# Two RMS norms of a one-core decoder layer: last output tiles and first products by halves of the tokens

## The chip, the cores and the metric

The kernel runs on one core of a Trainium2 chip. The metric is the device time of one execution in microseconds (us), from the first to the last instruction with what lies around them. Before the change the median of three runs is 1109.05 us (1107.43 to 1109.75).

## What is computed

The input x has 512 tokens of 1024 channels. Every product is in float32 accuracy.

```python
h = modulate(rms_norm(x, norm_ffn1), shift0, scale0)
x = x + 0.5 * gate0 * swiglu(h, w_ffn1_in, w_ffn1_out)      # D_FF = 2816
h = modulate(rms_norm(x, norm_mix), shift1, scale1)         # "norm 1" below
u_pool, q_lat, kv_lat, k_rope, g_pool, g_mla = split(h @ w_in)
...                                                         # pooling branch, latent attention, gates
x = x + gate1 * (merged @ w_out)
h = modulate(rms_norm(x, norm_ffn2), shift2, scale2)        # "norm 2" below
x = x + 0.5 * gate2 * swiglu(h, w_ffn2_in, w_ffn2_out)
```

`rms_norm` divides each token by the root of the mean of its squares over all 1024 channels. So a token can be normalised only when all its channels are complete.

## The kernel before

**Layout.** Activations lie with channels on the 128 partitions and tokens along the free axis: x, h_hi and h_lo are 8 tiles (index m or k) of 128 channels x 512 tokens. Each float32 value is split into a high and a low part, and every product is three TensorE matmuls (L433 to L435): high x high, high x low, low x high. Weights stream from HBM in chunks through two slots, w_raw, w_hi, w_lo [0] and [1]. ScalarE makes w_hi (L762, `split`), VectorE w_lo (L1098). A chunk can be split only when TensorE has finished with the chunk before it in the same slot.

**Order.** Each engine runs its own list of instructions, written out by hand, strictly in order. Semaphores link the lists: `wait_ge(sem, n)` stops an engine until another has counted that far, and everything behind it on that engine stops too. `lo_done` counts split chunks, `pe_used` chunks that TensorE has finished, `out_evac` tiles of x that are updated, `lat_ready` finished groups of latent products.

**The stretch around norm 1.** FFN 1 ends with the down projection. It makes the 8 tiles of x one after another (`down`). Tile m takes two chunks of 11 weight tiles (half 0 in slot 0, half 1 in slot 1): 2 x 11 x 3 = 66 matmuls of 512 columns. VectorE adds the result to x (L1592), ScalarE squares it (L771), GpSimd adds the squares up in ssq; VectorE adds the last square (L1116). Then TensorE sums over the partitions (L445: four matmuls of one column, one for each 128 tokens; float32, shown as two each), VectorE forms the variance (L1120), ScalarE the root (L775), VectorE the inverse root with one Newton step (L1125 to L1130) and a diagonal matrix (diag, L1137). TensorE spreads it over all partitions (L451, float32, 512 columns). For each m VectorE scales x (L1153), ScalarE adds the shift to give h_hi (L783), VectorE gives h_lo (L1161). `scaled` has two buffers. The first products behind it are the latents: three column groups cg (256, 256 and 160 columns) times four blocks of 128 tokens, here with h as the loaded operand and the weights as the moving one. Group 0 takes the k tiles as they come; groups 0 and 1 together are 192 matmuls of 256 columns. Chunk 0 of the mixer is split during the last down tile, chunk 1 (`mix_split(1)`) after the norm.

**The stretch around norm 2.** The output projection of the mixer makes the tiles of x with 24 matmuls each, two tiles to a chunk (`for c in range(4)`, evacuation L1517). The same chain follows, and then the up projection of FFN 2: chunk j gives one gate and one up tile, 2 x 8 x 3 = 48 matmuls of 512 columns. Its chunk 0 is split before norm 2, chunk 1 after it. After each chunk ScalarE takes silu (L980), VectorE multiplies (L1529), ScalarE and VectorE split the result (L982, L1531), and ScalarE and VectorE split the next chunk into the free slot.

**SP's queue** loads weights as slots come free; behind `stat_ready` of norm 1 it loads the mixer's constants.

## Time and profile before

| | |
|---|---|
| median of three runs | 1109.05 us (1107.43 to 1109.75) |
| the profiled execution | 1108.44 us |
| its span | 1106.3 us, 12576 instructions |
| TensorE matmul (PE) | 1061.5 us busy, 96% |
| VectorE (DVE) | 523.7 us, 47% |
| ScalarE (ACT) | 368.3 us, 33% |
| GpSimd (POOL) | 71.6 us, 6% |

The profile is of one execution. All its times count from the start of the span. PE's busy time counts overlapping matmuls once. "Idle before" is how long the engine stood before an instruction, and the name behind the arrow is what released it. In the view by stretch a row gives the stretch (us from the span's start), its length, then busy us and count for PE, PEld (weight load), DVE, ACT and POOL, then the granted TensorE clock (1.00 is 2.4 GHz, 0.50 is 1.2 GHz), the DMA share and GB/s. In the view in order of time a row gives start, duration, engine, line and operation.

### The profile page before, as it was taken

To read this page: it belongs to the slowest core of one execution; us is meant where nothing else is said; L and a number is where in the kernel's file an instruction comes from. 1 tells how busy PE (TensorE), PEld (TensorE's weight loads), DVE (VectorE), ACT (ScalarE), POOL (GpSimd) and SP (SyncE) were. 2 spreads that over 40 slices of the span, in tenths; PEclk is the share of its full clock that TensorE was granted. 3 is DMA by queue.
4 is the path that set the end of the run, shared out by engine and by line. 5 is a ranking of instruction groups with operands and counts; after the bars stand their busy time and mean duration, and the time that the engine had idled before them with its cause. 6 is when DMAs were issued, how large, how long until landed. Compare 5 with 4: busy or idle time off the path is not lost.

```text
span 1106.3 us, 12576 instructions
## 1 busy us (share of the span) xinstructions
PE 1061.5 (96%) x4860; PEld 874.5 (79%) x4860; DVE 523.7 (47%) x669; ACT 368.3 (33%) x498; POOL 71.6 (6%) x58
## 2 busy tenths in 40 slices
PE   3999999999999979979999999979999999999998
PEld 2888888888888869768788887858888888888886
DVE  5765564655553262758565455363323333322221
ACT  6532223232121232564444443232322323221110
POOL 0000000000000000850100004200000000000000
PEclk9999999999999989999999999989999999999999
DMA  9764545454763212222121222313232222222222
GB/s 353 293 249 157 224 164 217 176 192 157 245 238 104 102 51 97 91 73 79 39 76 38 76 75 78 114 38 114 76 114 81 109 91 98 90 79 87 95 86 94
DMA packets 28874, 138.56 MB, mean 125 GB/s; under 512 B 3248, under 2 KB 3504, under 8 KB 20912
## 3 DMA queue, kind: packets, MB, share of 16 engines
q1 hardware_dynamic: 28848, 138.23, 34.9%
q8 instruction: 15, 0.25, 0.1%
q14 instruction: 11, 0.09, 0.0%
HBM read 136.12 MB, written 2.10 MB: 125 GB/s over the span
## 4 chain that ended last, share of the span: by engine, by line
PE 90%; POOL 3%; DVE 3%; ACT 2%; DMA 1%; issue 1%; SPq 1%; ACTq 0%; DVEq 0%; POOLq 0%
PE bank L433 29%; PE bank L434 28%; PE bank L435 28%; PE bank L676 2%; POOL window L1674 1%; DMA ada_first<-w_ada 1%; PE bank L691 1%; ACT w_hi L762 1%; POOL window L1679 1%; PE bank L664 1%; POOL u_pad L1680 1%; DVE w_lo L1098 1%; POOL h L1703 0%; PE bank L451 0%; DVE mvar L1306 0%
## 5 line engine op out<-in xcount | busy, mean ns | idle before, releaser
L433 PE MATMUL bank<-h_hi,w_hi 128*128 128x512 f32 x928 | 365.8, 394 | 6.4 <-DVE h_lo L1205 2.8
L435 PE MATMUL bank<-h_lo,w_hi 128*128 128x512 f32 x928 | 363.0, 391 | 0.0
L434 PE MATMUL bank<-h_hi,w_lo 128*128 128x512 f32 x928 | 363.0, 391 | 0.0
L1098 DVE TENSOR_TENSOR w_lo<-w_raw,w_hi 128x2048 fp32r<-128x2048 f32 (+3 forms) x96 | 198.6, 2068 | 172.7 <-ACT w_hi L762 172.5
L433 PEld LDWEIGHTS bank<-h_hi,w_hi 128*128 128x128 f32 x928 | 175.3, 189 | 47.2 <-issue 6.1
L762 ACT ACTIVATE w_hi<-w_raw 128x2048 fp32r<-128x2048 f32 (+3 forms) x96 | 164.6, 1715 | 124.4 <-PE bank L435 72.2
L435 PEld LDWEIGHTS bank<-h_lo,w_hi 128*128 128x128 f32 x928 | 175.3, 189 | 37.3
L434 PEld LDWEIGHTS bank<-h_hi,w_lo 128*128 128x128 f32 x928 | 175.4, 189 | 35.8
L433 PE MATMUL bank<-act_hi,w_hi 128*128 128x512 f32 x352 | 139.2, 396 | 0.0
L434 PE MATMUL bank<-act_hi,w_lo 128*128 128x512 f32 x352 | 139.2, 396 | 0.0
L435 PE MATMUL bank<-act_lo,w_hi 128*128 128x512 f32 x352 | 139.2, 396 | 0.0
L980 ACT ACTIVATE scaled<-bank 128x512 f32<-128x512 f32 x44 | 26.3, 597 | 279.7 <-PE bank L435 279.7
L1529 DVE TENSOR_TENSOR scaled<-scaled,bank 128x512 f32<-128x512 f32 x44 | 30.3, 688 | 167.5 <-ACT scaled L980 167.5
L435 PEld LDWEIGHTS bank<-act_lo,w_hi 128*128 128x128 f32 x352 | 66.1, 188 | 16.0
L434 PEld LDWEIGHTS bank<-act_hi,w_lo 128*128 128x128 f32 x352 | 66.1, 188 | 16.0
L433 PEld LDWEIGHTS bank<-act_hi,w_hi 128*128 128x128 f32 x352 | 66.1, 188 | 16.0
L1103 DVE CUSTOM_DVE_ANT_0 ada_raw<-ada_raw,c_wide,const_sb 128x1024 f32<-128x1024 f32 x56 | 69.7, 1280 | 2.9 <-DMA ada_raw<-w_ada 2.9
L1531 DVE TENSOR_TENSOR act_lo<-scaled,act_hi 128x512 fp32r<-128x512 f32 (+1 forms) x44 | 30.5, 693 | 36.3 <-ACT act_hi L982 36.3
L1592 DVE SCALAR_TENSOR_TENSOR x<-bank,out_gate,x 128x512 f32<-128x512 f32 (+1 forms) x16 | 12.0, 751 | 68.4 <-PE bank L435 68.4
L982 ACT ACTIVATE act_hi<-scaled 128x512 f32 (+1 forms) x44 | 27.8, 632 | 39.6 <-DVE scaled L1529 39.6
L771 ACT ACTIVATE scaled<-x 128x512 f32<-128x512 f32 (+1 forms) x16 | 10.1, 632 | 84.7 <-DVE x L1592 57.2
L433 PE MATMUL bank<-w_hi,h_hi 128*128 128x256 f32 (+1 forms) x96 | 28.1, 293 | 2.6 <-DVE h_lo L1161 2.6
(182 smaller groups left out, 891.5 us busy)
## 6 DMA issues: line engine op xcount, KB each, us to landing
w_raw<-w_ffn_in SPq DMA_DIRECT2D x41, 1024.0 KB, 4.8
ada_raw<-w_ada SPq DMA_DIRECT2D x56, 512.0 KB, 5.4
w_raw<-w_ffn_out SPq DMA_DIRECT2D x32, 704.0 KB, 4.0
w_raw<-w_mix SPq DMA_DIRECT2D x21, 1024.0 KB, 4.8
ada_first<-w_ada SPq DMA_DIRECT2D x16, 512.0 KB, 12.7
w_raw<-w_ffn_in SPq DMA_DIRECT2D x6, 512.0 KB, 12.8
x_tok<-x_rows SPq DMA_DIRECT2D x4, 512.0 KB, 6.8
x<-x_t SPq DMA_DIRECT2D x4, 512.0 KB, 5.6
```

What stands on the lines that cost most here:

```text
L433: nc.tensor.matmul(dst, a_hi, b_hi, start=start, stop=False)
L434: nc.tensor.matmul(dst, a_lo, b_hi, start=False, stop=False)
L435: return nc.tensor.matmul(dst, a_hi, b_lo, start=False, stop=stop)
L676: nc.tensor.matmul(bank[qt][:, 0:(qt + 1) * P], q_now[0:HEAD, toks(qt)], k_t[0:HEAD, bass.ds(h, 1), 0:(qt + 1) * P], start=True, stop=False)
L762: nc.scalar.activation(w_hi[slot][:, 0:size], w_raw[slot][:, 0:size], ACT.Copy).then_inc(hi_done, 1)
L980: nc.scalar.activation(silu_g, bank[banks[0]][:, :], ACT.Silu).then_inc(silu_done, 1)
L982: nc.scalar.activation(act_hi[f][:, bass.ds(j, 1), :], prod, ACT.Copy).then_inc(act_hi_done, 1)
L1098: nc.vector.tensor_tensor(w_lo[slot][:, 0:size], w_raw[slot][:, 0:size], w_hi[slot][:, 0:size].bitcast(F32), ALU.subtract).then_inc(lo_don ...
L1103: nc.vector.tensor_tensor_reduce(out=raw, in0=raw, in1=c_wide[:, :], scale=1.0, scalar=bias_ada[:, col:col + 1], op0=ALU.mult, op1=ALU.add ...
L1529: nc.vector.tensor_tensor(prod, silu_g, bank[banks[1]][:, :], ALU.mult).then_inc(gu_evac, 1)
L1531: nc.vector.tensor_tensor(act_lo[f][:, bass.ds(j, 1), :], prod.unsqueeze(1), act_hi[f][:, bass.ds(j, 1), :].bitcast(F32), ALU.subtract)\
L1592: nc.vector.scalar_tensor_tensor(out=xm, in0=bank[4 + s // 2][:, :].unsqueeze(1), scalar=out_gate[:, bass.ds(m, 1)], in1=xm, op0=ALU.mult, ...
```

## The change

The tokens are cut into two halves of 256 (hf 0 and 1).

- The last down tile of FFN 1 (m = 7) and the last two tiles of the output projection (m = 6, 7) are made for half 0 first, then for half 1, each in a bank of its own.
- GpSimd adds up only the squares of the tiles before them. The squares of the halved tiles go to `sq_last`, and TensorE adds them in the sum over the partitions (`norm_sum`), which is made for each half. `norm_wide` spreads each half. Sum and spread of half 0 stand between products of half 1's tiles; those of half 1 between the first products that follow the norm.
- The first two latent groups, and the first two up chunks of FFN 2, take half 0 first and then half 1.
- ScalarE and VectorE work on 128 x 256. Their lists around the norms are written out anew (`norm_mix`, `norm_ffn2`), with the splits of mixer chunks 0 (as two parts, `mix_first`) and 1, and of up chunk 1, between the steps.
- Slots count as free at other points: mixer chunk 0 after 6 groups of latent products. SP loads the mixer's constants after the second sum.

In the diff below the first lists are TensorE's, `high`, `last_square`, `norm_std` are ScalarE's, and the last lists VectorE's; `half_out(m, hf, ...)` is the update of half a tile of x, `norm_var` the variance, `norm_diag` the root's inverse and diag.

```diff
+HALF = S // 2
+LAT_ORDER = [(0, 0), (0, 1), (1, 0), (1, 1), (0, 2), (0, 3), (1, 2), (1, 3), (2, 0), (2, 1), (2, 2), (2, 3)]
+SQUARES_BY_POOL = [0, 7, 13]
+RSTD_BANK = [None, (4, 7), (6, 7)]
...
+        scaled_half = [scaled[:, i // 2, HALF * (i % 2):HALF * (i % 2) + HALF] for i in range(4)]
+        sq_last = place("sq_last", [P, 2, 2, HALF], at=phase_at)
+        diag = place("diag", [P, 2, HALF], at=phase_at + 4096)
...
-            sp.wait_ge(stat_ready, 1)
+            sp.wait_ge(stat_ready, 2)
...
+            def norm_sum(l, hf):
+
+                pe.wait_ge(sq_added, SQUARES_BY_POOL[l])
+                pe.wait_ge(sq_last_done, hf + 1 if l == 1 else 2 + 2 * hf + 2)
+                for t in (2 * hf, 2 * hf + 1):
+                    col = STAT_BANK[:, t:t + 1]
+                    nc.tensor.matmul(col, ssq[:, t * P:(t + 1) * P], ones[:, 0:1], start=True, stop=False)
+                    for mm in range(l):
+                        last = nc.tensor.matmul(col, sq_last[:, hf, mm, t % 2 * P:(t % 2 + 1) * P], ones[:, 0:1],
+                                                start=False, stop=mm == l - 1)
                 last.then_inc(stat_ready, 1)

-            def norm_wide(l):
-                pe.wait_ge(diag_ready, l)
-                nc.tensor.matmul(bank[4][:, :], ones, diag, start=True, stop=True).then_inc(rstd_wide, 1)
+            def norm_wide(l, hf):
+                pe.wait_ge(diag_ready, 2 * (l - 1) + hf + 1)
+                nc.tensor.matmul(bank[RSTD_BANK[l][hf]][:, half_cols(hf)], ones, diag[:, hf, :], start=True, stop=True)\
+                    .then_inc(rstd_wide, 1)
...
+                def up_by_halves():
+
+                    for s in range(2):
+                        pe.wait_ge(lo_done, n0 + s + 1)
+                        pe.wait_ge(gu_evac, NF + s + 1)
+                        for k in range(KD):
+                            if s == 0:
+                                pe.wait_ge(half_ready[0], KD + k + 1)
+                            up_half(s, 0, k)
+                            if s == 0 and k == 2:
+                                norm_sum(2, 1)
+                            if s == 0 and k == 4:
+                                norm_wide(2, 1)
+                    for s in range(2):
+                        for k in range(KD):
+                            if s == 0:
+                                pe.wait_ge(half_ready[1], KD + k + 1)
+                            last = up_half(s, 1, k)
+                        last.then_inc(pe_used, 1)
...
+                def down_last():
+
+                    for half in range(2):
+                        pe.wait_ge(lo_done, n0 + NF + 14 + half + 1)
+                    pe.wait_ge(out_evac, KD + 1 - 1)
+                    for hf in range(2):
+                        for half in range(2):
+                            for k in range(NFH):
+                                cols = half_cols(hf)
+                                last = product(bank[5 + hf][:, cols], w_tile(half, k),
+                                               (act_hi[0][:, half * NFH + k, cols], act_lo[0][:, half * NFH + k, cols]),
+                                               half + k == 0, half * k == NFH - 1)
+                                if hf == 1 and half == 0 and k == 5:
+                                    norm_sum(1, 0)
+                            if hf:
+                                last.then_inc(pe_used, 1)
+                                if half == 0:
+                                    norm_wide(1, 0)
+                            elif half:
+                                last.then_inc(tail_done, 1)
...
+                if f == 0:
+                    with pe.Fori(0, 3) as i:
+                        down(i)
+                    down(3, 1)
+                    down_last()
...
+                for k in range(KD):
+                    if k < 4:
+                        pe.wait_ge(half_lo_done, 2)
+                    else:
+                        chunk(LAT_AT)
+                    pe.wait_ge(half_ready[0], k + 1)
+                    for t in range(2):
+                        lat_part(t, k, 0, t)
+                    if k == 2:
+                        norm_sum(1, 1)
+                    if k == 4:
+                        norm_wide(1, 1)
+                chunk(LAT_AT + 1)
+                for t in range(2):
+                    for k in range(KD):
+                        lat_part(2 + t, k, 1, t)
+                for k in range(KD):
+                    pe.wait_ge(half_ready[1], k + 1)
+                    for t in range(2):
+                        lat_part(4 + t, k, 0, 2 + t)
+                for t in range(2):
+                    for k in range(KD):
+                        lat_part(6 + t, k, 1, 2 + t)
+                chunk(LAT_AT + 2)
+                for t in range(TOK):
+                    pe.wait_ge(lat_evac, t + 1)
+                    for k in range(KD):
+                        lat_part(8 + t, k, 2, t)
...
+                slot = chunk(WOUT_AT + 3)
+                for hf in range(2):
+                    for g in range(2):
+                        pe.wait_ge(out_evac, KD + 6 + 2 * hf + g - 1)
+                        at = (6, 7, 4, 5)[2 * hf + g]
+                        for k in range(KD):
+                            last = product(bank[at][:, half_cols(hf)], w_tile(slot, g * KD + k), h_pair(k, half_cols(hf)),
+                                           k == 0, k == KD - 1)
+                            if (hf, g, k) == (1, 0, 5):
+                                norm_sum(2, 0)
+                            if (hf, g, k) == (1, 1, 2):
+                                norm_wide(2, 0)
+                        if hf and g:
+                            last.then_inc(pe_used, 1)
+                        else:
+                            last.then_inc(tail_done, 1)
...
+            def norm_mix():
+
+                last_square(1, 0, 7, 1)
+                norm_std(1, 0)
+                mix_first(0)
+                high(1, 0, 0)
+                high(1, 0, 1)
+                mix_first(1)
+                high(1, 0, 2)
+                last_square(1, 1, 7, KD + 2)
+                high(1, 0, 3)
+                norm_std(1, 1)
+                high(1, 0, 4)
+                high(1, 0, 5)
+                high(1, 0, 6)
+                mix_split(1)
+                high(1, 0, 7)
...
-                                         bias=mod[:, shift + m:shift + m + 1]).then_inc(h_hi_ready, 1)
+                    high(1, 1, m)
...
+            def scale_in(l, hf, m):
+
+                if m >= 2:
+
+                    dve.wait_ge(half_ready[hf], KD * (l - 1) + m - 1)
+                nc.vector.scalar_tensor_tensor(out=scaled_half[2 * hf + m % 2], in0=x[:, m, half_cols(hf)],
+                                               scalar=gain_mod[:, m:m + 1], in1=bank[RSTD_BANK[l][hf]][:, half_cols(hf)],
+                                               op0=ALU.mult, op1=ALU.mult).then_inc(half_scaled[hf], 1)
+
+            def low(l, hf, m):
+
+                dve.wait_ge(half_scaled[hf], KD * (l - 1) + m + 1)
+                dve.wait_ge(half_high[hf], KD * (l - 1) + m + 1)
+                nc.vector.scalar_tensor_tensor(out=h_lo[:, m, half_cols(hf)], in0=scaled_half[2 * hf + m % 2],
+                                               scalar=mod[:, 3 * KD * l + m:3 * KD * l + m + 1],
+                                               in1=h_hi[:, m, half_cols(hf)].bitcast(F32), op0=ALU.add, op1=ALU.subtract)\
+                    .then_inc(half_ready[hf], 1)
...
+            def norm_mix():
+
+                dve.wait_ge(ada_step, ADA_TILES - ADA_START)
+                gain_cols(1)
+                dve.wait_ge(tail_done, 1)
+                half_out(7, 0, 5, tail_evac)
+                norm_var(1, 0)
+                norm_diag(1, 0)
+                dve.wait_ge(rstd_wide, 1)
+                scale_in(1, 0, 0)
+                scale_in(1, 0, 1)
+                mix_first(0)
+                low(1, 0, 0)
+                scale_in(1, 0, 2)
+                low(1, 0, 1)
+                mix_first(1)
+                dve.wait_ge(pe_used, FFN_CHUNKS)
+                half_out(7, 1, 6, out_evac)
+                scale_in(1, 0, 3)
+                low(1, 0, 2)
+                norm_var(1, 1)
+                scale_in(1, 0, 4)
+                low(1, 0, 3)
+                norm_diag(1, 1)
+                scale_in(1, 0, 5)
+                low(1, 0, 4)
+                scale_in(1, 0, 6)
+                low(1, 0, 5)
+                scale_in(1, 0, 7)
+                low(1, 0, 6)
+                mix_split(1)
+                low(1, 0, 7)
+                dve.wait_ge(rstd_wide, 2)
+                scale_in(1, 1, 0)
...
+                        scale_in(1, 1, m + 1)
+                    low(1, 1, m)
...
+            def norm_ffn2():
+
+                gain_cols(2)
+                for g in range(2):
+                    dve.wait_ge(tail_done, 2 + g)
+                    half_out(6 + g, 0, 6 + g, tail_evac)
+                norm_var(2, 0)
+                norm_diag(2, 0)
+                dve.wait_ge(tail_done, 4)
+                half_out(6, 1, 4, out_evac)
+                dve.wait_ge(rstd_wide, 3)
+                scale_in(2, 0, 0)
+                scale_in(2, 0, 1)
+                low(2, 0, 0)
+                scale_in(2, 0, 2)
+                low(2, 0, 1)
+                dve.wait_ge(pe_used, FFN_CHUNKS + 4)
+                half_out(7, 1, 5, out_evac)
+                scale_in(2, 0, 3)
+                low(2, 0, 2)
+                norm_var(2, 1)
+                scale_in(2, 0, 4)
+                low(2, 0, 3)
+                norm_diag(2, 1)
+                scale_in(2, 0, 5)
+                low(2, 0, 4)
+                scale_in(2, 0, 6)
+                low(2, 0, 5)
+                split(FIRST_CHUNK[1] + 1, 1, IN_ELEMS)
+                scale_in(2, 0, 7)
+                low(2, 0, 6)
+                low(2, 0, 7)
+                dve.wait_ge(rstd_wide, 4)
+                scale_in(2, 1, 0)
```

## Rows read from the trace of the kernel before

**Rows 1.** page: busy us, share of the span, instructions of each engine.

```profile
PE 1061.5 (96%) x4860; PEld 874.5 (79%) x4860; DVE 523.7 (47%) x669; ACT 368.3 (33%) x498; POOL 71.6 (6%) x58
```

**Rows 2.** busy time by stretch, around norm 1 and around norm 2.

```profile
373.63:389.03 15.40, 15.40 (x67) 12.21 (x65) 4.67 (x3) 3.82 (x3) 1.30 (x1) 1.00 0.19 68
389.03:399.26 10.23, 3.27 (x11) 1.50 (x11) 5.31 (x13) 2.31 (x5) 0.47 (x4) 0.76 0.28 85
399.26:424.74 25.48, 25.48 (x193) 25.48 (x194) 15.95 (x31) 9.94 (x15) 0.00 (x0) 0.89 0.24 84
...
716.72:727.61 10.89, 10.89 (x49) 8.82 (x47) 3.71 (x3) 3.07 (x3) 2.60 (x2) 1.00 0.27 96
727.61:737.77 10.16, 3.29 (x12) 1.50 (x11) 5.31 (x13) 3.70 (x6) 0.00 (x0) 0.73 0.00 0
737.77:761.88 24.11, 24.11 (x96) 19.73 (x97) 15.07 (x17) 9.20 (x10) 0.00 (x0) 0.90 0.25 88
```

**Rows 3.** TensorE in order of time in norm 1 (start, us, operation).

```profile
391.52 1.02 PE L445 MATMUL bank<-ones_r,ssq 128*128 128x1 f32 x8 [2.32 <-DVE ssq L1116]
394.56 2.07 PE L451 MATMUL bank<-scaled,ones_r 128*128 128x512 f32 x2 [2.02 <-DVE scaled L1137]
```

**Rows 4.** VectorE and ScalarE in order of time in norm 1.

```profile
389.24 0.75 DVE L1592 SCALAR_TENSOR_TENSOR x<-bank,out_gate,x 128x512 f32<-128x512 f32 x1 [3.40 <-PE bank L435]
...
390.02 0.63 ACT L771 ACTIVATE scaled<-x 128x512 f32<-128x512 f32 x1 [6.51 <-DVE x L1592]
...
393.82 0.69 DVE L1137 TENSOR_TENSOR scaled<-const_sb,rstd 128x512 f32<-128x512 f32 x1
...
396.76 1.41 DVE L1153 SCALAR_TENSOR_TENSOR scaled<-x,gain_mod,bank 128x512 f32<-128x512 f32 x2 [2.17 <-PE bank L451]
...
397.54 1.38 ACT L783 ACTIVATE h_hi<-scaled,mod 128x512 fp32r<-128x512 f32 x2 [4.46 <-DVE scaled L1153]
...
398.37 0.75 DVE L1161 SCALAR_TENSOR_TENSOR h_lo<-scaled,mod,h_hi 128x512 fp32r<-128x512 f32 x1 [0.20 <-ACT h_hi L783]
```

**Rows 5.** the latent products of 256 columns at full clock, by stretch.

```profile
405.00:424.68 19.68, 19.68 (x166) 19.68 (x166) 10.35 (x23) 7.04 (x11) 0.00 (x0) 1.00 0.31 107
```

**Rows 6.** groups by line and form: busy us, mean ns, idle before.

```profile
L1098 DVE TENSOR_TENSOR w_lo<-w_raw,w_hi 128x2048 fp32r<-128x2048 f32 x61 | 141.2, 2315 | 82.3 <-ACT w_hi L762 82.2
L762 ACT ACTIVATE w_hi<-w_raw 128x2048 fp32r<-128x2048 f32 x61 | 116.5, 1910 | 5.2 <-PE bank L435 5.1
...
L783 ACT ACTIVATE h_hi<-scaled,mod 128x512 fp32r<-128x512 f32 x16 | 11.5, 725 | 16.7 <-DVE scaled L1153 16.7
...
L1466 DVE TENSOR_TENSOR p_lo<-bank,p_hi 128x512 fp32r<-128x512 f32 x16 | 10.3, 687 | 26.7 <-ACT p_hi L792 26.7
L792 ACT ACTIVATE p_hi<-bank 128x512 fp32r<-128x512 f32 x16 | 8.7, 599 | 0.0
...
L1466 DVE TENSOR_TENSOR p_lo<-bank,p_hi 128x256 fp32r<-128x256 f32 x8 | 3.3, 415 | 0.0
...
L792 ACT ACTIVATE p_hi<-bank 128x256 fp32r<-128x256 f32 x8 | 3.2, 402 | 0.0
```

**Rows 7.** VectorE and ScalarE in order of time behind down tile 6.

```profile
373.84 0.75 DVE L1592 SCALAR_TENSOR_TENSOR x<-bank,out_gate,x 128x512 f32<-128x512 f32 x1 [4.60 <-PE bank L435]
376.56 1.63 DVE L1098 TENSOR_TENSOR w_lo<-w_raw,w_hi 128x1408 fp32r<-128x1408 f32 x1 [1.97 <-ACT w_hi L762]
...
375.16 1.36 ACT L762 ACTIVATE w_hi<-w_raw 128x1408 fp32r<-128x1408 f32 x1
```

**Rows 8.** ScalarE's silu of up chunk 0, FFN 2, and VectorE's next split.

```profile
751.20 0.60 ACT L980 ACTIVATE scaled<-bank 128x512 f32<-128x512 f32 x1 [3.00 <-PE bank L435]
...
755.10 2.29 DVE L1098 TENSOR_TENSOR w_lo<-w_raw,w_hi 128x2048 fp32r<-128x2048 f32 x1 [1.12 <-ACT w_hi L762]
```

**Rows 9.** TensorE's stop before 494.57, and the stretch 493 to 494.

```profile
494.57 0.77 PE L433 MATMUL bank<-group_hi,w_hi 128*128 128x512 f32 x1 [4.29 <-DVE group_lo L1389]
...
493.00:494.00 1.00, 0.00 (x0) 0.00 (x0) 1.00 (x2) 1.00 (x3) 1.00 (x1) 0.70 0.00 0
```

More of the change, by code:

```diff
@@ L460, in up_part, with up @@
                     return last
-                def up(i, first):
+                def up(i):
                     for s in range(2):
@@ L538, in first_up, with up_half @@
                     last.then_inc(pe_used, 1)
+                def up_half(s, hf, k):
+                    for gu in range(2):
+                        last = product(bank[2 * s + gu][:, half_cols(hf)], w_tile(s, gu * KD + k),
+                                       (h_hi[:, k, half_cols(hf)], h_lo[:, k, half_cols(hf)]), k == 0, k == KD - 1)
+                    return last
+                def up_by_halves():
[16 more added lines that the diff above has]
+                        last.then_inc(pe_used, 1)
                 if f == 0:
@@ L577, in mixer, with lat_part @@
             def mixer():
[L580 to L592 removed]
+                def lat_part(r, k, cg, t):
+                    n = LAT_COLS[cg][1]
+                    last = product(bank[r % 8][:, 0:n], h_pair(k, toks(t)), w_cols((MIX_CHUNK + cg) % 2, k * n, n),
+                                   k == 0, k == KD - 1)
+                    if k == KD - 1:
+                        last.then_inc(lat_ready, 1)
+                for k in range(KD):
[26 more added lines that the diff above has]
+                        lat_part(8 + t, k, 2, t)
                 for c in range(2):
@@ L728, in mixer @@
                 pe.wait_ge(merged_ready, 2)
-                for c in range(4):
+                for c in range(3):
                     slot = chunk(WOUT_AT + c)
@@ new lines, in last_square, with norm_std @@
+            def last_square(l, hf, m, count):
+                if hf:
+                    act.wait_ge(out_evac, count)
+                else:
+                    act.wait_ge(tail_evac, count)
+                nc.scalar.activation(sq_last[:, hf, m - (8 - l), :], x[:, m, half_cols(hf)], ACT.Square)\
+                    .then_inc(sq_last_done, 1)
+            def norm_std(l, hf):
+                act.wait_ge(var_ready, 2 * (l - 1) + hf + 2)
+                nc.scalar.activation(std[:, 2 * hf:2 * hf + 2], var[:, 2 * hf:2 * hf + 2], ACT.Sqrt).then_inc(std_ready, 1)
@@ new lines, in norm_ffn2 @@
+            def norm_ffn2():
+                last_square(2, 0, 6, 2)
+                last_square(2, 0, 7, 3)
+                norm_std(2, 0)
+                last_square(2, 1, 6, 2 * KD + 1)
+                high(2, 0, 0)
+                high(2, 0, 1)
+                high(2, 0, 2)
+                last_square(2, 1, 7, 2 * KD + 2)
+                high(2, 0, 3)
+                norm_std(2, 1)
+                high(2, 0, 4)
+                high(2, 0, 5)
+                split(FIRST_CHUNK[1] // 2, 1, IN_ELEMS, (pe_used, FFN_USED[1]))
+                high(2, 0, 6)
+                high(2, 0, 7)
+                for m in range(KD):
+                    high(2, 1, m)
+                load_table(4, ACT.Silu)
@@ new lines, in rsqrt_cols @@
+            def rsqrt_cols(n, cols):
+                dve.wait_ge(std_ready, n)
+                r, w, v = rstd[:, cols], newton[:, cols], var[:, cols]
+                link(nc.vector.reciprocal(r, std[:, cols]))
+                link(nc.vector.tensor_tensor(w, r, r, ALU.mult))
+                link(nc.vector.scalar_tensor_tensor(out=w, in0=w, scalar=-0.5, in1=v, op0=ALU.mult, op1=ALU.mult))
+                return nc.vector.scalar_tensor_tensor(out=r, in0=w, scalar=1.5, in1=r, op0=ALU.add, op1=ALU.mult)
@@ new lines, in half_out, with mix_first @@
+            def half_out(m, hf, at, done):
+                cols = half_cols(hf)
+                nc.vector.scalar_tensor_tensor(out=x[:, m, cols], in0=bank[at][:, cols], scalar=out_gate[:, m:m + 1],
+                                               in1=x[:, m, cols], op0=ALU.mult, op1=ALU.add).then_inc(done, 1)
+            def mix_first(part):
+                dve.wait_ge(hi_done if part else half_hi_done, MIX_CHUNK + 1 if part else 2)
+                n = MIX_SIZES[0] // 2
+                cols = slice(n * part, n * part + n)
+                nc.vector.tensor_tensor(w_lo[0][:, cols], w_raw[0][:, cols], w_hi[0][:, cols].bitcast(F32), ALU.subtract)\
+                    .then_inc(lo_done if part else half_lo_done, 1)
@@ L1548, in first_up, with step @@
                     gated(2, 2, first_banks[2])
-                def step(j, s, last):
-                    split(n0 + j + 1, 1 - s, OUT_ELEMS if last and s else IN_ELEMS)
+                def step(j, s, last, loaded=False):
+                    if not loaded:
+                        split(n0 + j + 1, 1 - s, OUT_ELEMS if last and s else IN_ELEMS)
                     if f == 0:
```

198 lines of the change are left out of this document (78 added, 120 removed).

## Prediction

> **What bounds the kernel now.** I read the busy times first: TensorE is busy 96% of the span, VectorE 47%, ScalarE 33% [rows 1]. So nearly everything TensorE does counts in full, and so does every wait of TensorE. Next I read busy time by stretch around the two norms [rows 2]. In front of norm 1 the last down tile takes 15.40 us at full clock. Then come 10.23 us without useful products, then 192 products of 256 columns in 25.48 us at a granted clock of 0.89. Around norm 2 it is 10.89 us for 48 products, a gap of 10.16 us, and 24.11 us for 96 products at 0.90. The TensorE rows of the first gap show what it holds: wait, sum of squares (1.02 us), wait, spread of rstd (2.07 us), wait [rows 3]. Between them stands a chain on VectorE and ScalarE in which each step waits for the one before [rows 4].
>
> The change can only win what a gap costs. Norm 1: 10.23 us, and the slow clock behind it. Products of 256 columns come every 0.120 us at full clock (19.68 us for 164) [rows 5], so 192 are worth 23.04 us; 2.4 us were lost. Together 12.7 us. Norm 2: 96 products at 10.89/48 = 0.227 are worth 21.8 us, 2.3 us were lost, with the gap 12.5 us. On the table: 25.2 us.
>
> **The prices.** Half-wide operations: VectorE 687 to 415 ns, so 256 columns are worth 0.27 us; ScalarE 599 to 402, 0.20 us [rows 6]. Hence 0.48 us for a half of scaling, of h_lo or of an output tile (0.75 [rows 4] less 0.27), 0.53 us for a half of h_hi (0.725 [rows 6] less 0.20), 0.43 for a half square (0.63 less 0.20 [rows 4]), 0.42 for a half diag, 1.23 and 1.1 us for half of the first mixer chunk (2.32 less 4 x 0.27, 1.91 less 4 x 0.20). One after another on one engine they follow 0.08 us earlier than they end, since two wide scalings take 1.41 us and not 1.50 [rows 4]. From an engine's end to the next one's start 0.03 us (x at 389.24 + 0.75, square at 390.02), ScalarE to VectorE 0.1, to TensorE 0.14, from the last product to its reader 0.2.
>
> **TensorE's own extra work.** (a) Splitting. Down tile 7: 66 products become 132. Its wide ones come every 15.40/66 = 0.233 us, 0.020 above 512 columns at 2.4 GHz; I give the halves the same 0.020, 0.127 each: +1.3 us. Bounds: 0.117 (exactly half, +0) and 0.14 (+3). Norm 2 splits 48 + 96 = 144 products at 0.227 into 288 at 0.120: +1.9 us (bounds 0 and 4). (b) Sums and spreads now stand between products. Four one-column products took 1.02 us at full clock [rows 3]; norm 1 issues two sets of four, norm 2 two of six (two squares outside ssq): 2.0 and 3.0 us. The spread took 2.07 us at the low clock, 512 wide; half of it at full clock is a quarter, 0.52, and 0.44 without its tail, which runs beside the next products: 0.9 us at each norm. Bounds for one spread 0.4 to 1.0. All of it: 4.2 us at norm 1, 5.8 us at norm 2.
>
> A rule on (a), which nothing else here uses: the Trainium skill (TensorE: Matmul & The Clock Gate, Back-to-back issue gap) adds about 2.5 ns to columns over 2.4 GHz. By it 210 more products would be an estimated 0.5 us, and by the rows (0.120 us where 256 columns at 2.4 GHz are 0.107 [rows 5]) it is 3.2 us with the down tile's 20. The row decides.
>
> **Where TensorE waits in the changed kernel.** I walked all queues in order with these prices.
>
> *Before down tile 7* (new). Its first half of the tokens needs both weight chunks, so TensorE waits for both before its first product. The second chunk takes the slot that tile 6 frees at 373.63. VectorE takes x of tile 6 at 373.84, ScalarE squares it and splits the chunk from 375.16, VectorE from 376.56 until 378.19 [rows 7]. Today this is hidden behind the tile's first 7.7 us. Now TensorE stands from 373.63 to 378.33: **4.7 us**. Nothing in the diff moves that split.
>
> *Norm 1*, times from that restart. First half done 8.4; x half 8.6, square, summed by 11.6 (TensorE is busy meanwhile). var, std, rstd and diag end at 13.5, TensorE ready for the spread at 13.55: 0.1 us. Scaling starts at 14.3. On VectorE the two half splits of chunk 0 (1.2 us each) stand between the first scalings, so TensorE, done with the tile at 18.3, waits for the second until 18.9: 0.6 us. Tiles 0 to 2 go; then the second sum, until 22.1. VectorE stands at var, which waits for that sum; behind it are the scaling of 4 and h_lo of 3. TensorE gets h_lo 3 at 23.3: 1.3 us. diag (five linked operations) is ahead of h_lo 4: 1.2 us. Behind h_lo 6 comes chunk 1: ScalarE 1.91 us, VectorE 2.32 us [rows 6], ahead of h_lo 7. VectorE ends it at 30.4, h_lo 7 at 30.8; TensorE waits from 27.8 to 30.9: **3.1 us**. From there it is fed: second-half tiles come every 0.9 us, with 5.8 us of chunk 1 products in hand. Waits: 4.7 + 0.1 + 0.6 + 1.3 + 1.2 + 3.1 = 11.0 us.
>
> *Norm 2*, from the first product of output tile 6 (716.72). The first spread waits 0.2 us, the three first input tiles 0.8 in all, tile 3 behind the sum 1.3, tile 4 behind diag 1.2. The split of the second up chunk stands ahead of h_lo 6 (and of the scaling of 7): VectorE has it from 23.3 to 25.6, TensorE waits from 23.2 to 26.5: **3.3 us**. Then a wait that was hidden: up chunk 2 needs slot 0, freed now only 48 half products (5.8 us) before it is wanted, where it was 10.9. From silu's start (751.20) to the split's end (755.10 + 2.29) it takes 6.2 us [rows 8], with handovers 6.5: 0.8 us. Waits: 7.6 us.
>
> The four bigger waits hang on which instruction stands first in VectorE's queue; with half-wide operations 0.06 us cheaper or 0.07 dearer the walk gives 1.6 us less or 1.9 more over both norms. SP's queue: the mixer constants wait for the second sum, at about 400 instead of 392.5 (391.52 + 1.02 [rows 3]), and are wanted only after the second half's h_lo, at 416; the angle work behind it ends before chunk 2's turn. Nothing there.
>
> **Sum.** Norm 1: 11.0 + 4.2 - 12.7 = +2.5 us. Norm 2: 7.6 + 5.8 - 12.5 = +0.9 us. All later work hangs on TensorE and moves with it (the pooling on GpSimd too, since it starts from products). At full clock: **+3.4 us**.
>
> *The clock.* TensorE idled 4.29 us before 494.57, and the clock was already at half for the last part of 493 to 494 (mean 0.70); no stop of 2.3 us (before 391.52) brought it down by itself [rows 9, 3]. After the gaps it stayed low for about 5 us of work, which cost 2.3 to 2.4 us each. The 4.7 us stand is longer than the 4.29 that brought it down; the 3.1 and 3.3 us lie between the two rows. I give the first a chance of 0.6 and the others 0.35 each, and take one fall: +2.5 us. Forecast +5.9 us; on the profiled 1108.44 us that is 1114.3, on the median of 1109.05 it is 1115.0.
>
> **Rivals.**
> *No fall*: the same walk, +3.4 us, 1112.4. For it: two stops of 2.3 and 2.0 us passed at full clock [rows 3] before it fell. Against it: the 4.29 us stop.
> *Two or three falls*: +8.4 or +10.9 us, 1117.5 to 1120. For it: in each norm 1.3, 1.2 and 3 us of waits follow closely.
> *The overlap holds*: the weight splits in the queues don't reach TensorE. Price: without the 3.1 and 3.3 us and with no fall, 3.4 - 6.4 = -3.0 us, 1106; with no wait at all but the 4.7 us, 4.2 + 5.8 + 4.7 - 25.2 = -10.5 us, 1098.6. It decides the sign when all waits together are under 15.2 us, where I have 18.6. For it: VectorE is busy only half the time; against it: it is the order of its queue, not its load, that holds h_lo 7 and h_lo 6 back.
> *It doesn't do what it says*, down tile 7 starting without its second chunk: excluded, both waits stand ahead of the first product.
>
> **How the numbers follow.** One fall 0.40, none 0.22, two or three 0.25, overlap holds 0.08, operations cheaper throughout (walk at +1, no fall) 0.05. The range reaches from the cheap end of no fall (+1.8 less a little) to two falls and three in part: 1110 to 1120. A measurement tells 0.2%, 2.2 us, from no change. Faster by more: 0.06, all from the overlap. Within: 0.11, from its weak end, the cheap operations and some of no fall. Slower: 0.83.
>
> **What would show it.** Right: a TensorE wait of about 4.7 us on the w_lo of the last down chunk; waits of about 3 us on h_lo just after a 2048-wide split on VectorE at both norms; useful products resuming within 1 us of the last half tile; the 192 latent products ending about 5 us later than 424.74 [rows 2], 2.5 of them the clock's; granted clock 0.5 for some 5 us after 378. Wrong: half products spaced under 0.11 us, or no wait before down tile 7, or a first h_lo wait over 2 us.

## The result and the profile after

Before: median 1107.87 us of 19 runs (1106.63 to 1109.75). Changed: median 1111.81 us of 19 (1109.22 to 1113.18). The ratio is 1.0033 (95% interval 1.0026 to 1.0039): 3.7 us slower, 2.9 to 4.3. That is the sign that was forecast and inside the range, 2.2 us under the forecast difference of 5.9. The profiled execution took 1112.51 us, span 1110.7 us; the one before 1108.44 and 1106.3. So the two profiles are 4.1 to 4.4 us apart, near the medians.

The page of the changed kernel (busy us, share of the span, instructions), to be held against [rows 1]:

```profile
PE 1067.3 (96%) x5098; PEld 890.5 (80%) x5098; DVE 529.3 (48%) x715; ACT 372.8 (34%) x519; POOL 70.1 (6%) x56
```

TensorE has 238 more matmul instructions and is busy 5.8 us longer, although two gaps of 10 us are gone: what was idle is now slower or additional work and new waits. Busy time by stretch of the changed kernel, with the columns of [rows 2] (a count also takes in the product that runs on into the stretch, so it can be one too high):

```profile
372.89:377.54 4.65, 0.17 (x2) 0.04 (x1) 2.45 (x3) 1.90 (x2) 1.27 (x1) 0.89 0.00 0
377.54:383.41 5.87, 5.87 (x28) 5.87 (x29) 0.00 (x0) 0.00 (x0) 0.00 (x0) 0.50 0.50 179
383.41:399.08 15.67, 15.17 (x129) 14.88 (x128) 7.31 (x17) 4.91 (x9) 0.00 (x0) 1.00 0.00 1
399.08:427.49 28.41, 25.10 (x190) 24.51 (x191) 18.89 (x49) 11.28 (x23) 0.37 (x3) 0.94 0.26 81
719.39:734.93 15.54, 15.32 (x123) 14.77 (x121) 9.04 (x20) 6.10 (x11) 1.30 (x1) 1.00 0.19 69
734.93:745.16 10.23, 6.60 (x38) 5.97 (x39) 6.67 (x15) 3.93 (x7) 0.00 (x0) 0.83 0.00 0
745.16:748.53 3.37, 3.37 (x16) 3.37 (x16) 2.85 (x7) 1.51 (x4) 0.00 (x0) 0.50 0.84 297
748.53:766.22 17.69, 17.09 (x143) 16.89 (x142) 8.32 (x14) 7.64 (x11) 0.00 (x0) 1.00 0.02 5
...
403.85:405.00 1.15, 1.15 (x5) 1.15 (x6) 1.11 (x3) 0.75 (x2) 0.00 (x0) 0.50 0.95 374
738.18:742.95 4.77, 4.39 (x20) 3.84 (x20) 3.52 (x10) 2.81 (x4) 0.00 (x0) 0.64 0.00 0
```

From the start of down tile 7's slot to the end of the 192 latent products these are 54.6 us (427.49 - 372.89). Before they were 51.1 (424.74 - 373.63) [rows 2]: **+3.5 us at norm 1**. From output tile 6 to the third up chunk it is 46.8 us (766.22 - 719.39) against 45.2 (761.88 - 716.72) [rows 2]: **+1.7 us at norm 2**. The kernel in front of norm 1 is 0.7 us shorter (372.89 against 373.63), between and behind the norms it is equal within 0.1. So 5.2 - 0.7, the 4.4 us between the spans with rounding. The clock is the thing to see in the rows: 0.50 behind the stand (TensorE's long wait before down tile 7), and low again from 403.85, from 738.18 and from 745.16, by the spacing of the products until about 407.3, 741.7 and 748.5. By the means of the rows it is low for some 17 us around the two norms, where it was some 21 before [rows 2]. So it is not low for longer; what matters is which work now falls under it.

TensorE in order of time (start, us, operation, idle before and what released it). The first five rows are the waits of norm 1, the sixth (of 160 columns) is the first product behind the 192 latents, and the last three are the longer waits of norm 2 (two more, of 0.21 and 0.37 us, are not shown):

```profile
377.54 0.55 PE L441 MATMUL bank<-act_hi,w_hi 128*128 128x256 f32 x1 [4.48 <-DVE w_lo L1261]
...
399.08 0.35 PE L441 MATMUL bank<-w_hi,h_hi 128*128 128x256 f32 x1 [0.50 <-DVE h_lo L1324]
...
401.94 0.36 PE L441 MATMUL bank<-w_hi,h_hi 128*128 128x256 f32 x1 [1.13 <-DVE h_lo L1324]
...
403.85 0.55 PE L441 MATMUL bank<-w_hi,h_hi 128*128 128x256 f32 x1 [0.96 <-DVE h_lo L1324]
...
409.43 0.35 PE L441 MATMUL bank<-w_hi,h_hi 128*128 128x256 f32 x1 [1.22 <-DVE h_lo L1324]
...
427.49 0.24 PE L441 MATMUL bank<-w_hi,h_hi 128*128 128x160 f32 x1
...
738.18 0.47 PE L441 MATMUL bank<-h_hi,w_hi 128*128 128x256 f32 x1 [1.04 <-DVE h_lo L1324]
...
745.16 0.58 PE L441 MATMUL bank<-h_hi,w_hi 128*128 128x256 f32 x1 [2.21 <-DVE h_lo L1324]
...
766.22 0.49 PE L441 MATMUL bank<-h_hi,w_hi 128*128 128x512 f32 x1 [0.60 <-DVE w_lo L1261]
```

A row's idle time begins at the end of the product before it, which lies some 0.15 us behind the point where the next could have started. Counted from that point the three waits in the middle of norm 1 are 0.66, 1.27 and 1.12 us. VectorE, in order of time, shows why the waits before 409.43 and 745.16 are there: a 2048-wide weight split stands in front of the h_lo that TensorE wants. The last h_lo below starts at 408.81, although its scaled input was there at 405.13:

```profile
404.65 0.48 DVE L1316 SCALAR_TENSOR_TENSOR scaled<-x,gain_mod,bank 128x256 f32<-128x256 f32 x1
405.05 0.48 DVE L1324 SCALAR_TENSOR_TENSOR h_lo<-scaled,mod,h_hi 128x256 fp32r<-128x256 f32 x1
406.60 2.29 DVE L1261 TENSOR_TENSOR w_lo<-w_raw,w_hi 128x2048 fp32r<-128x2048 f32 x1 [1.07 <-ACT w_hi L864]
408.81 0.48 DVE L1324 SCALAR_TENSOR_TENSOR h_lo<-scaled,mod,h_hi 128x256 fp32r<-128x256 f32 x1
```

VectorE stands 1.07 us for ScalarE's part of the split, which in ScalarE's list is ahead of the same tile's h_hi, and then works 2.29 us on its own part. It is busy 48% of the span; its order causes the wait, not its load.

TensorE's first sum over the partitions and its first spread, each between two products:

```profile
389.89 0.28 PE L458 MATMUL bank<-ones_r,ssq 128*128 128x1 f32 x2
390.03 0.36 PE L460 MATMUL bank<-ones_r,sq_last 128*128 128x1 f32 x2
390.25 0.36 PE L458 MATMUL bank<-ones_r,ssq 128*128 128x1 f32 x2
390.47 0.36 PE L460 MATMUL bank<-ones_r,sq_last 128*128 128x1 f32 x2
390.70 0.36 PE L441 MATMUL bank<-act_hi,w_hi 128*128 128x256 f32 x1
390.90 0.28 PE L442 MATMUL bank<-act_hi,w_lo 128*128 128x256 f32 x1
...
392.57 0.70 PE L466 MATMUL bank<-diag,ones_r 128*128 128x256 f32 x2
392.92 0.47 PE L441 MATMUL bank<-act_hi,w_hi 128*128 128x256 f32 x1
393.22 0.28 PE L442 MATMUL bank<-act_hi,w_lo 128*128 128x256 f32 x1
```

The next product starts 0.81 us behind the start of the sum (390.70 - 389.89) and 0.35 us behind that of the spread (392.92 - 392.57). That product is itself slower than its 0.12 us: the one after it starts 0.20 and 0.30 us later. So the sum costs 0.89 us in all (390.90 - 389.89 - 0.12) and the spread 0.53 (393.22 - 392.57 - 0.12).

### The profile page after: what moved, and what is told of

Its sections match the earlier page's. It is cut to its first block, busy times and chain, and to the rows that moved or that the text cites. A ratio compares the mean times of both kernels' runs of the same rounds, so it can differ in the third digit from the quotient of the medians.

```text
span 1110.7 us, 13126 instructions
## 1 busy us (share of the span) xinstructions
PE 1067.3 (96%) x5098; PEld 890.5 (80%) x5098; DVE 529.3 (48%) x715; ACT 372.8 (34%) x519; POOL 70.1 (6%) x56
## 4 chain that ended last, share of the span: by engine, by line
PE 88%; DVE 4%; POOL 3%; ACT 2%; issue 2%; DMA 1%; SPq 1%; ACTq 0%; POOLq 0%; DVEq 0%
PE bank L441 28%; PE bank L443 28%; PE bank L442 28%; PE bank L765 2%; ACT w_hi L864 1%; POOL window L1909 1%; DMA ada_first<-w_ada 1%; DVE w_lo L1261 1%; PE bank L780 1%; POOL window L1914 1%; PE bank L753 1%; POOL u_pad L1915 1%; DVE scaled L1316 0%; POOL h L1938 0%; DVE h_lo L1324 0%
## 5 line engine op out<-in xcount | busy, mean ns | idle before, releaser
L441 PE MATMUL bank<-h_hi,w_hi 128*128 128x512 f32 (+1 forms) x976 | 375.4, 385 | 8.0 <-DVE h_lo L1324 3.8
L443 PE MATMUL bank<-h_lo,w_hi 128*128 128x512 f32 (+1 forms) x976 | 371.8, 381 | 0.0
L442 PE MATMUL bank<-h_hi,w_lo 128*128 128x512 f32 (+1 forms) x976 | 371.6, 381 | 0.0
L1261 DVE TENSOR_TENSOR w_lo<-w_raw,w_hi 128x2048 fp32r<-128x2048 f32 (+2 forms) x95 | 196.2, 2065 | 164.4 <-ACT w_hi L864 164.3
L441 PEld LDWEIGHTS bank<-h_hi,w_hi 128*128 128x128 f32 x976 | 185.3, 190 | 46.1 <-DVE h_lo L1324 4.6
L442 PEld LDWEIGHTS bank<-h_hi,w_lo 128*128 128x128 f32 x976 | 185.5, 190 | 34.0
L864 ACT ACTIVATE w_hi<-w_raw 128x2048 fp32r<-128x2048 f32 (+2 forms) x95 | 162.6, 1711 | 119.0 <-PE bank L443 66.9
L441 PE MATMUL bank<-act_hi,w_hi 128*128 128x512 f32 (+1 forms) x374 | 143.9, 385 | 4.5 <-DVE w_lo L1261 4.5
L442 PE MATMUL bank<-act_hi,w_lo 128*128 128x512 f32 (+1 forms) x374 | 143.5, 384 | 0.0
L443 PE MATMUL bank<-act_lo,w_hi 128*128 128x512 f32 (+1 forms) x374 | 143.4, 384 | 0.0
L443 PEld LDWEIGHTS bank<-act_lo,w_hi 128*128 128x128 f32 x374 | 71.3, 191 | 15.2
## 6 DMA issues: line engine op xcount, KB each, us to landing
ada_first<-w_ada SPq DMA_DIRECT2D x16, 512.0 KB, 12.7
```

Source lines behind the costliest of these rows:

```text
L441: nc.tensor.matmul(dst, a_hi, b_hi, start=start, stop=False)
L442: nc.tensor.matmul(dst, a_lo, b_hi, start=False, stop=False)
L443: return nc.tensor.matmul(dst, a_hi, b_lo, start=False, stop=stop)
L864: nc.scalar.activation(w_hi[slot][:, 0:size], w_raw[slot][:, 0:size], ACT.Copy).then_inc(hi_done, 1)
L1261: nc.vector.tensor_tensor(w_lo[slot][:, 0:size], w_raw[slot][:, 0:size], w_hi[slot][:, 0:size].bitcast(F32), ALU.subtract).then_inc(lo_don ...
```

## Experiments

Each was timed beside the kernel before, whose median there was 1108.2 to 1108.3 us. Differences are given from the ratios: the changed kernel stands at +3.7 us (1.0033). A difference between two versions has both their intervals in it, about 1.1 to 1.5 us either way.

**The stand before down tile 7, taken away.** The changed kernel, with the second chunk waited for where it is first used:

```diff
                 def down_last():
-                    for half in range(2):
-                        pe.wait_ge(lo_done, n0 + NF + 14 + half + 1)
                     pe.wait_ge(out_evac, KD + 1 - 1)
                     for hf in range(2):
                         for half in range(2):
+                            if hf == 0:
+                                pe.wait_ge(lo_done, n0 + NF + 14 + half + 1)
```

> The changed kernel, with TensorE's wait for the second chunk of down tile 7 moved from before the tile to before the first product that uses it. Theory (the 4.5 us stand before tile 7 is that wait, and it brings the clock down for about 6 us of products, worth 2.7 us): 33 half products (3.7 us) run before the stand, 0.9 us of it is left, the clock stays up: 6.4 us less than the changed kernel, about 1105.5 us, 2.5 us under the kernel before. Rival (the stand costs its length only, the clock would have fallen a little later anyway): 3.7 us less, no change against before. Rival (the stand is slack given back at the norm, where VectorE is late): less than 1.5 us less.

Measured: 1106.3 us (1103.52 to 1107.33), ratio 0.9978 (0.9969 to 0.9987): 2.4 us faster than before, 6.1 under the changed kernel. The wait shrinks from 4.48 to 0.69 us, and the clock of the same stretch stays up:

```profile
377.98 0.39 PE L441 MATMUL bank<-act_hi,w_hi 128*128 128x256 f32 x1 [0.69 <-DVE w_lo L1261]
```

```profile
373.40:377.98 4.58, 3.89 (x34) 3.70 (x33) 2.43 (x3) 1.91 (x2) 1.30 (x1) 1.00 0.00 0
```

3.8 of the 6.1 us are the wait, and 2.3 (1.1 to 3.5) are left for the clock. In the two profiles the whole of it lies at norm 1: the stretch from tile 7 to the end of the latents is 6.5 us shorter, that of norm 2 the same within 0.1. This one wait decides the sign of the whole change.

**The stand alone.** The kernel before, its down tile 7 whole as it was; only TensorE waits for both chunks first:

```diff
-                def down(i):
+                def down(i, early=False):
                     for mm in range(2):
                         m = 2 * i + mm
+                        if early and mm == 1:
+                            pe.wait_ge(lo_done, n0 + NF + 2 * m + 2)
```

> The kernel before, with one thing of the change alone: TensorE waits for both chunks of down tile 7 of FFN 1 before it starts the tile. Theory (stand plus clock): +4.6 us of stand and +2.5 us of slow clock, 7.1 us over before, 1115. Rival (stand alone): +4.6 us. Rival (the time comes back at norm 1): under +1.5 us; nothing there has slack in this kernel, since each step waits for the one before.

Measured: 1114.39 us (1112.27 to 1115.3), ratio 1.0055 (1.0042 to 1.0068): +6.1 us. Its rows, TensorE's first product of tile 7 and the stretches around it:

```profile
378.61 0.79 PE L433 MATMUL bank<-act_hi,w_hi 128*128 128x512 f32 x1 [4.43 <-DVE w_lo L1105]
...
382.02 0.39 PE L435 MATMUL bank<-act_lo,w_hi 128*128 128x512 f32 x1
```

```profile
374.00:378.61 4.61, 0.18 (x2) 0.01 (x1) 2.38 (x2) 1.90 (x2) 1.27 (x1) 0.98 0.00 0
378.61:383.00 4.39, 4.39 (x13) 3.49 (x14) 0.00 (x0) 0.00 (x0) 0.00 (x0) 0.64 0.66 239
```

4.6 us are the stand, 1.5 the rest; by the interval of the time alone the rest could be anything from 0.1 to 2.9. The profile says what it is: from 378.61 to 382.02 there are 8 products, 3.41 us where 8 x 0.233 = 1.87 were due [rows 2], so 1.5 us were lost to the clock. The stand lowers the clock in a kernel that has nothing else of the change.

**VectorE's queue.** The changed kernel, with VectorE's two big splits moved behind the last h_lo of the first half, and ScalarE's parts moved ahead of the second root:

```diff
                 low(1, 0, 6)
-                mix_split(1)
                 low(1, 0, 7)
+                mix_split(1)
...
-                split(FIRST_CHUNK[1] + 1, 1, IN_ELEMS)
                 scale_in(2, 0, 7)
                 low(2, 0, 6)
                 low(2, 0, 7)
+                split(FIRST_CHUNK[1] + 1, 1, IN_ELEMS)
```

> The changed kernel; at both norms VectorE's 2048-wide weight split is moved from ahead of h_lo 7 (norm 1) and h_lo 6 (norm 2) to behind h_lo 7, and ScalarE's part of it into the time in which ScalarE waits for the second variance. Theory (the order in VectorE's queue makes TensorE wait for these tiles): the waits of 1.2 us (norm 1) and 2.2 us (norm 2) go, with the slow clock behind the second; 4 to 5 us less than the changed kernel, 1107.3 us, about 0.5 us under before. Rival (the split is needed as early as that, and TensorE only waits for w_lo instead): under 1 us less.

Measured: 1108.28 us (1107.52 to 1110.21), ratio 1.0004 (0.9995 to 1.0013): no different from before, 3.2 us under the changed kernel. Both waits on h_lo behind the splits are gone. In their place stand shorter ones on the split itself, at norm 1 and at norm 2:

```profile
408.37 0.39 PE L441 MATMUL bank<-w_hi,h_hi 128*128 128x256 f32 x1 [0.36 <-DVE w_lo L1261]
...
743.12 0.39 PE L441 MATMUL bank<-h_hi,w_hi 128*128 128x256 f32 x1 [0.51 <-DVE w_lo L1261]
```

The expected gain was 4 to 5 us; 3.2 us with both intervals is 2.0 to 4.4, so the shortfall is hardly clear of the noise. The two new waits take back 0.9 us. A part may be something that the old waits had hidden: in the changed kernel the clock is low from 403.85 and from 738.18, and a TensorE that works slowly towards a wait that ends when VectorE is ready loses nothing. With the waits gone the clock is still low there (0.73 and 0.81 in the rows), and the slow products count. Busy time by stretch of this kernel, first behind the stand:

```profile
378.31:381.40 3.09, 3.09 (x14) 3.09 (x15) 0.00 (x0) 0.00 (x0) 0.00 (x0) 0.50 0.64 225
402.50:408.00 5.50, 5.01 (x30) 4.49 (x28) 5.18 (x9) 1.52 (x3) 0.00 (x0) 0.73 0.38 128
738.00:743.00 5.00, 4.30 (x27) 4.00 (x26) 4.68 (x8) 1.46 (x3) 0.00 (x0) 0.81 0.00 0
```

How much of the shortfall is hidden slowness and how much is chance, this run doesn't tell. The last version below bears on it.

**Both edits together.**

> The late wait of down tile 7 (e1) and the moved splits (e2) together. Theory (two separate stretches of TensorE's path): the two gains add, 6.1 and 3.2 us off the changed kernel, so 5.6 us under the kernel before, about 1102.5. Rival (they share the clock: part of e2's gain was slow products that e1 had already turned fast, or the other way round): 3 to 4 us under before.

Measured: 1101.99 us (1100.41 to 1102.89), ratio 0.994 (0.9926 to 0.9953): 6.6 us faster than before, 10.3 under the changed kernel, where the two edits sum to 6.1 + 3.2 = 9.3. They add up within the noise, so the waits are separate losses; the rival, that part of one gain is the other's over again and only 3 to 4 us are won, falls.

**The change at norm 1 alone.** Norm 2, its output tiles and first up chunks are as before.

> The change at norm 1 alone; norm 2, its output tiles and the first up chunks as in the kernel before. Theory (the traces: norm 1 gains 3.5 and norm 2 1.7 of 5.2 us in the profiled executions, 3.9 us in the median): +2.6 us over before, 1110.5; norm 2's part is the remaining 1.3. Prediction's split: +2.5 and +0.9 at full clock. Rival (norm 2 carries most, its waits on VectorE being longer): +1 or less.

Measured: 1110.81 us (1108.6 to 1112.11), ratio 1.0024 (1.0014 to 1.0034): +2.7 us. By subtraction norm 2's part is +1.0, which the two intervals leave anywhere between -0.3 and 2.3: norm 1's part loses, norm 2's can't be told from nothing.

**What a split of a product costs.** The kernel before, with all 528 products of FFN 2's down tiles made as two of 256 columns, each half in its own bank, and x updated in two halves:

```diff
                             for k in range(NFH):
-                                last = product(bank[4 + mm][:, :], w_tile(half, k),
+                                for hf in range(1 + f):
+                                    cols = slice(S // 2 * hf, S // 2 * hf + S // (1 + f))
+                                    last = product(bank[4 + mm + 2 * hf][:, cols], w_tile(half, k),
...
```

> The kernel before, with all 8 down tiles of FFN 2 made from products of 256 columns (1056 for 528), two for each weight tile, in two banks, and added to x in two halves; nothing else. It prices splitting alone. By the prediction (0.127 us a half against 0.233): +10 to +11 us. By norm 1's latents (0.120): +3.5 us. By the changed kernel's down tile 7 (0.1133 at full clock while VectorE was idle): -3.5 us.

Measured: 1109.32 us (1108.08 to 1111.36), ratio 1.0015 (1.0006 to 1.0024): +1.7 us, 3 ns for each of 528 splits (1 to 5). Forty microseconds of the down tiles, first of this kernel, then of the one before:

```profile
985.00:1025.00 40.00, 40.00 (x340) 40.00 (x339) 9.88 (x9) 6.91 (x5) 0.00 (x0) 1.00 0.31 107
```

```profile
985.00:1025.00 40.00, 40.00 (x174) 32.18 (x173) 9.63 (x7) 6.91 (x5) 0.00 (x0) 1.00 0.32 108
```

A half comes every 40/340 = 0.118 us, a whole every 40/174 = 0.230, which makes some 5 ns a split in these executions, the upper end of what the medians allow. The 0.127 that the prediction gave a half of an act product would have been 528 x 0.021, some 11 us here.

**A version that is faster than either kernel.** The changed kernel with the late wait; in VectorE's lists the second variance stands behind h_lo 4 of the first half, the weight split behind its last h_lo, and diag behind the split; ScalarE's lists follow; TensorE's second spread comes later, between products that are already supplied. VectorE's list of norm 1 (norm 2 likewise):

```diff
-                norm_var(1, 1)
                 scale_in(1, 0, 4)
                 low(1, 0, 3)
-                norm_diag(1, 1)
                 scale_in(1, 0, 5)
                 low(1, 0, 4)
+                norm_var(1, 1)
                 scale_in(1, 0, 6)
                 low(1, 0, 5)
                 scale_in(1, 0, 7)
                 low(1, 0, 6)
-                mix_split(1)
                 low(1, 0, 7)
+                mix_split(1)
+                norm_diag(1, 1)
```

> e5's two edits, and VectorE's second variance and diag moved behind h_lo 4 and behind the weight split, TensorE's second spread behind the first 24 products of mixer chunk 1 (norm 1) or half of up chunk 1's first half (norm 2). Theory (the two waits of about 1.1 and 0.9 us at tiles 3 and 4 come from instructions ahead in VectorE's queue, not from its load): these waits fall to 0.2 us each, 2 us less at each norm than e5; 9 us under before, about 1099. Rival (VectorE has no time left there: 0.9 us a tile against TensorE's 0.72, so the waits come back at later tiles): within 1.5 us of e5.

Measured: 1099.21 us (1097.66 to 1099.7), ratio 0.9916 (0.9903 to 0.993): **9.3 us faster than before**, 13.0 under the changed kernel. TensorE's waits (engine, line, waited for: us in total, times, longest), from 365 to 425 us:

```profile
PE bank L441 <- DVE w_lo L1261: 1.9, 2, 1.2
PE bank L441 <- DVE h_lo L1324: 0.5, 1, 0.5
```

In the changed kernel there were 8.3 us in that place. In this profile the granted clock is 1.00 in each stretch of 10 us from 372 to 430 and from 715 to 765, and 0.997 over the span, against 0.989 in the changed kernel's.

Against the version with both edits the median is 2.8 us lower and the span of the profile 3.4 us. TensorE's idle time around the two norms falls by only 0.7 us between the two profiles (from 3.3 and 2.1 us to 2.4 and 2.3). The clock is what differs: with both edits it was still low for some 14 us there, here it never is. With both edits:

```profile
390.00:400.00 10.00, 7.44 (x47) 6.82 (x47) 7.62 (x20) 5.01 (x9) 0.37 (x3) 0.80 0.29 89
400.00:410.00 10.00, 10.00 (x75) 10.00 (x74) 9.14 (x19) 5.04 (x12) 0.00 (x0) 0.86 0.29 105
...
725.00:735.00 10.00, 8.49 (x50) 7.47 (x49) 7.21 (x21) 5.66 (x10) 0.00 (x0) 0.78 0.00 0
735.00:745.00 10.00, 10.00 (x76) 10.00 (x75) 9.28 (x18) 4.40 (x9) 0.00 (x0) 0.88 0.30 107
```

So most of this last step's gain is products that ran slowly before and don't now. That is the evidence for slow products that count once no wait lies behind them.

## Why the prediction was right, and where it was off

**The mechanism held.** The halves do fill both gaps: useful products resume within 1 us of the last half tile, and 12.7 and 12.5 us come free. All of it is spent again, by what was named: the wait before down tile 7 and the slow clock behind it, the order of VectorE's queue, and TensorE's own extra work. Two of the signs that were to show it came smaller: the waits behind the 2048-wide splits are 1.2 and 2.2 us by their rows and not about 3, and the 192 latent products end 2.8 us later than before (427.49 against 424.74) and not 5.

**The walk through the queues, norm 1.** The stand: 4.7 forecast, 4.65 measured. The following waits: 0.6, 1.3 and 1.2 forecast; 0.66, 1.27 and 1.12 measured. The spread of half 0 was put at a wait of 0.1 and had none. The last: 3.1 forecast. The row shows an idle of only 1.22 (1.38 from the point where the next product could have started), since the clock fell at 403.85 and the products and the spread in front of it took 1.5 us longer; together 2.9. VectorE's half-wide operations took 0.48 for h_lo and 0.42 for diag, as priced. At norm 2 the three first input tiles were put at 0.8 us and show 0.21, tile 3 at 1.3 (1.17 from the point where it could have started), the third up chunk at 0.8 (0.60 by its row).

**Sums and spreads: nearly right, by two small errors.** With the slower product behind it, a sum cost 0.89 us at norm 1 where 1.0 was taken, and 1.33 at norm 2 (727.31 to 728.76, less 0.12) where 1.5 was; the second sum of each norm is followed by a wait and cost 0.80 and 1.25. A spread cost 0.53 at full clock where 0.44 was taken. The forecast had left out the spread's tail as running beside the next products, but the product behind it starts a slow 0.30 us. Four one-column products cost less between products than in a gap, where they took 1.02 [rows 3]. In all 2.8 us instead of 2.9 at norm 1, and 3.6 instead of 3.9 at norm 2.

**Down tile 7 split: mis-sized, 1.5 us.** The prediction took 0.127 us for a half, +1.3 us for the tile. The 132 halves and what stands between them show 0.113 to 0.118 at full clock, about 15.2 us for the tile against the 15.40 of [rows 2]. The error is in carrying over 0.020 us above the columns' time from a wide product to each half; the lower bound, exactly half, was nearly right. The test on 528 products confirms it (3 ns each, not 20). At norm 2 and for the latents the halves came at the forecast 0.120, so this was one term, not the method. The rule that the prediction weighed here, of the Trainium skill (TensorE: Matmul & The Clock Gate, Back-to-back issue gap), makes an estimated 2.5 ns for a split. The 3 ns of the test agree with it for these products; the 13 ns (0.120 twice, against 0.227) of products with h do not.

**The clock: the step that failed, in its count.** The prediction said: "take one fall: +2.5 us". It did not fall once. In the profile it was low four times, behind the stand, from 403.85, from 738.18 and from 745.16. The price was hung on the number of falls, as though each cost the same. What it costs depends on what TensorE does while it lasts:
- behind the stand nothing covers it: 2.8 us in the changed kernel's profile (27 products in 5.87 us, where 0.113 each were due), but 1.5 in each of three other profiles with the same stand (the stand alone; VectorE's queue, 14 products in 3.12 us; norm 1 alone), and 1.5 and 2.3 by the medians of the two experiments on it;
- from 403.85 and from 738.18 it lies in front of a wait on VectorE that would have been there anyway, and shortens it by what the slow products take longer: by 1.5 us at the first (1.4 are left), by some 1.3 at the second (2.2 are left by the idle row);
- from 745.16 to 748.53, 15 products took 3.37 us instead of 1.80: 1.6 us.

The rival "two or three falls" (1117.5 to 1120) was thus nearer in its count and wrong in its time. The rival "no fall" (+3.4 us, 1112.4) came nearest to the measured +3.7 and is wrong in its mechanism.

**The sums.** Norm 1: 4.65 + 3.05 + 2.9 of waits, 2.8 of sums and spreads, 2.8 of clock behind the stand, -0.2 for tile 7, less 12.7: +3.3, where the stretches say +3.5. The first product behind each of three waits, which takes 0.20 us and not 0.12, makes up the rest. Forecast was +5.0 with the fall. Norm 2: with 1.9 for the halves and 3.6 for sums and spreads, 1.7 + 12.5 - 5.5 = 8.7 us remain for waits and slow clock, 4.4 of them idle by the rows and 2.9 slow products. Forecast were 7.6, and no fall there.

Held against the forecast of 5.9 us, the 5.2 us of the two stretches are made of errors of opposite sign: tile 7 is 1.5 less, the waits are 0.9 less, sums and spreads 0.4 less, and the slow clock that nothing covers is 1.9 more (2.8 + 1.6 against 2.5); that gives 5.0, and the slower products behind waits 0.2. That the sum comes so near is in part luck. The median difference is smaller still, 3.7 us. The stretch in front of norm 1, 0.7 us shorter in this profile, and the 1.3 us between a loss of 2.8 and of 1.5 behind the stand show how much one execution can be off. In the medians norm 1 is +2.7 and norm 2 +1.0, smaller than in this one execution.

**The overlap rival** (chance 0.08) did not come, and what it hung on was rightly seen: with the stand nearly gone the kernel is faster than before, and with VectorE's order mended too it is 9.3 us faster. The statement that "nothing in the diff moves that split" was true; what should be added is that TensorE need not wait for it.

Open: why halves of act products come every 0.113 to 0.118 us and halves of h products every 0.120; and what sets the length of a slow stretch, which was 5.9 us behind the stand in the changed kernel's profile and some 3 us behind the same stand in three others.

## What to carry to other kernels

When work is cut into halves, look at what the first half needs whole: here both weight chunks, whose wait had been hidden in the tile, stood bare in front of it, and it alone turned a gain into a loss. In a queue that runs in order, put what the critical engine waits for first and large preparation behind it; here an engine at 48% busy held TensorE up by its order alone, and two moved splits won 3.2 us. Price a slow clock by what lies behind it: in front of a wait on another engine that would have come anyway it costs almost nothing here, and what removes that wait uncovers it.

## What the hardware showed that was not expected

- Splitting a 512-column product cost 3 ns (528 splits, +1.7 us in the median). Down tile 7 as 132 halves took no longer than as 66 wholes (about 15.2 us against 15.40, sums and spreads taken off).
- A float32 spread of 256 columns between two products cost 0.53 us, 0.18 of it in the product behind it, which took 0.30 us until the next.
- The clock fell not only in a stand of 4.5 us. It also fell at 403.85, after waits of 1.13 and 0.96 us with 0.8 us of work between them, and at 738.18, after 1.04 us.
- Of four profiled executions with nearly the same stand (4.43 to 4.48 us) one lost 2.8 us afterwards and three lost 1.5.
